# A two-layer decoder trunk on one core: the boundaries between sub-layers taken by token halves

## What is computed

```python
def rms_norm(x, g):
    y = x * lax.rsqrt(jnp.mean(x * x, axis=-1, keepdims=True) + NORM_EPS)
    return y * g

def swiglu(h, w_in, w_out):              # D_FF = 2816
    gu = h @ w_in
    gate, up = gu[..., :D_FF], gu[..., D_FF:]
    return (jax.nn.silu(gate) * up) @ w_out

for i in range(DEPTH):                   # DEPTH = 2
    f = swiglu(rms_norm(h, norm_pre[i, 0]), w_ffn_in[i, 0], w_ffn_out[i, 0])
    h = h + 0.5 * rms_norm(f, norm_post[i, 0])
    t = rms_norm(h, norm_pre[i, 1])
    t = attention(t) if i == 0 else conformer_conv_module(t)
    h = h + rms_norm(t, norm_post[i, 1])
    f = swiglu(rms_norm(h, norm_pre[i, 2]), w_ffn_in[i, 1], w_ffn_out[i, 1])
    h = h + 0.5 * rms_norm(f, norm_post[i, 2])
```

## Time and profile before

| | us |
|---|---|
| median of 3 runs | 1892.01 (1891.94 to 1893.06) |
| the profiled execution | 1891.92 |
| its span, first to last instruction | 1890.0 |
| PE busy | 1869.1 (99%) |
| weight loads of PE busy | 1542.6 (82%) |
| DVE busy | 1005.7 (53%) |
| ACT busy | 634.6 (34%) |
| POOL busy | 28.0 (1%) |

### The profile page before, as it was taken

How to read it: one execution, slowest core, us unless ns; L and a number is a source line. 1 busy time by engine, 2 the same in 40 slices (tenths; PEclk the granted TensorE clock), 3 DMA queues, 4 the chain that set the end, 5 groups by cost and what they waited for, 6 DMA issues and landing times.

```text
span 1890.0 us, 24212 instructions
## 1 busy us (share of the span) xinstructions
PE 1869.1 (99%) x8970; PEld 1542.6 (82%) x8970; DVE 1005.7 (53%) x1377; ACT 634.6 (34%) x920; POOL 28.0 (1%) x54
## 2 busy tenths in 40 slices
PE   8999999999999999999999999999999999999998
PEld 6888888887688888888888888888998888888886
DVE  5534434588766434444754344457767674344345
ACT  5322322446734222223442222234113543222223
POOL 0000000021000000000000000000000000000000
PEclk9999999999999999999999999999999999999999
DMA  5332223321023322323232232332332222322221
GB/s 189 111 100 100 89 100 100 114 84 62 14 88 100 100 90 99 100 90 106 72 122 90 99 101 90 99 111 76 124 121 96 89 78 89 100 100 96 94 100 56
DMA packets 62096, 181.49 MB, mean 96 GB/s; under 512 B 7088, under 2 KB 16448, under 8 KB 62032
## 3 DMA queue, kind: packets, MB, share of 16 engines
q1 hardware_dynamic: 60432, 179.09, 28.2%
q0 software_dynamic: 1600, 1.51, 0.3%
HBM read 173.63 MB, written 6.29 MB: 95 GB/s over the span
## 4 chain that ended last, share of the span: by engine, by line
PE 96%; DVE 2%; ACT 1%; DMA 1%; issue 0%; SPq 0%; DVEq 0%; ACTq 0%
PE bank L362 27%; PE bank L364 27%; PE bank L363 27%; PE bank L662 3%; PE bank L403 3%; PE bank L404 2%; PE bank L407 2%; PE bank L379 1%; PE bank L611 1%; PE bank L595 1%; PE bank L386 1%; PE bank L576 1%; DVE h_resid L1088 0%; DVE f_out L1083 0%; PE bank L552 0%
## 5 line engine op out<-in xcount | busy, mean ns | idle before, releaser
L977 DVE TENSOR_TENSOR w_lo<-w_raw,w_hi 128x1024 fp32r<-128x1024 f32 x307 | 375.3, 1225 | 449.0 <-ACT w_hi L745 438.6
L362 PE MATMUL bank<-x_hi,w_hi 128*128 128x512 f32 x1448 | 565.7, 391 | 0.8 <-DVE gate_tmp L1013 0.2
L364 PE MATMUL bank<-x_hi,w_lo 128*128 128x512 f32 x1448 | 563.5, 389 | 0.0
L363 PE MATMUL bank<-x_lo,w_hi 128*128 128x512 f32 x1448 | 563.4, 389 | 0.0
L745 ACT ACTIVATE w_hi<-w_raw 128x1024 fp32r<-128x1024 f32 x307 | 322.9, 1055 | 598.8 <-PE bank L364 596.8
L362 PE MATMUL bank<-a_hi,w_hi 128*128 128x512 f32 (+1 forms) x844 | 320.7, 380 | 0.4 <-DVE w_lo L977 0.4
L362 PEld LDWEIGHTS bank<-x_hi,w_hi 128*128 128x128 f32 x1448 | 271.8, 188 | 59.0 <-DVE gate_tmp L1013 2.1
L364 PE MATMUL bank<-a_hi,w_lo 128*128 128x512 f32 (+1 forms) x844 | 319.9, 379 | 0.0
L363 PE MATMUL bank<-a_lo,w_hi 128*128 128x512 f32 (+1 forms) x844 | 319.9, 379 | 0.0
L364 PEld LDWEIGHTS bank<-x_hi,w_lo 128*128 128x128 f32 x1448 | 271.8, 188 | 56.7
L363 PEld LDWEIGHTS bank<-x_lo,w_hi 128*128 128x128 f32 x1448 | 271.9, 188 | 55.6
(11 more groups left out here) (167 smaller groups left out, 1261.7 us busy)
## 6 DMA issues: line engine op xcount, KB each, us to landing
w_raw<-stream SPq DMA_DIRECT2D x312, 512.0 KB, 3.4
h_resid<-xT SPq DMA_DIRECT2D x8, 256.0 KB, 6.8
w_raw<-stream SPq DMA_DIRECT2D x8, 256.0 KB, 6.4
u_scratch<-V SPq DMA_DIRECT2D x8, 256.0 KB, 2.1
u_groups<-u_scratch SPq DMA_DIRECT2D x8, 256.0 KB, 2.8
qT<-z_scratch SPq DMA_DIRECT2D x8, 256.0 KB, 3.8
outT<-h_resid SPq DMA_DIRECT2D x8, 256.0 KB, 2.2
z_scratch<-kT SPq DMA_DIRECT2D x4, 256.0 KB, 2.3
```

The lines of the kernel that those rows point to most:

```text
L362: nc.tensor.matmul(out, lw[0], lx[0], start=first, stop=False)
L363: nc.tensor.matmul(out, lw[0], lx[1], start=False, stop=False)
L364: return nc.tensor.matmul(out, lw[1], lx[0], start=False, stop=last)
L977: nc.vector.tensor_tensor(w_lo[:, s, :], raw[:, s, :], w_hi[:, s, :].bitcast(F32), ALU.subtract).then_inc(s_lo, 1)
```

## The change

The last two down slots of every sub-layer but the last are made in the order: slot 7 tokens A (0 to 255), slot 8 A, slot 7 tokens B (256 to 511), slot 8 B (`last_two`), A in banks 6 and 7, B in banks 0 and 1. The sums of squares of the post norm, their root, the inverse and the broadcast are made for A and for B apart, those of A between products of the B halves, those of B between upper products of A of the next sub-layer (`first_four`). DVE scales and adds all eight chunks of A, then all eight of B, each 256 wide, and only then makes all `x_lo`, then adds the squares. PE makes the hi by hi and lo by hi products of the next four slots for all of A, then for all of B, then the products with `x_lo`, 512 wide. Of these four slots the third and fourth lie in two side buffers, `side_hi` and `side_lo`, since the ring places are still in use by the last two down slots. The four slots write banks 6, 7, 2 and 3. The filler matmuls of the boundaries are gone. The sums for `r_pre` are made in slot five ahead of its chunk 3, its broadcast ahead of its chunk 6; DVE adds the last square too, so there are four summing matmuls in place of eight. `u_groups` is laid into `a_lo`, to make room; its memset moves behind the last down slot ahead of the convolution.

On PE, with the buffers:

```diff
+        side_hi, side_lo = sb("w_side_hi", [P, 2, SLOT], F32R), sb("w_side_lo", [P, 2, SLOT], F32R)
...
-        ug = sb("u_groups", [P, 2, GROUPS, PAD + NT])
+        al = a_lo[:, :, :].bitcast(F32).rearrange("p a n -> p (a n)")
+        ug = al[:, 0:2 * GROUPS * (PAD + NT)].rearrange("p (i g n) -> p i g n", i=2, g=GROUPS)
...
+            def first_four(n0, sub):
...
+                def upper(k, tok):
+                    for s in range(RING):
...
+                        for part in range(2):
+                            nc.tensor.matmul(bank[FIRST_BANKS[s]][:, tok], w[KD * s + k][part], x_hi[:, k, tok],
+                                             start=(k == 0 and tok == A and part == 0), stop=False,
+                                             skip_group_check=True)
...
+                for k in range(KD):
+                    pe.wait_ge(s_xa, KD * (sub - 1) + k + 1)
+                    upper(k, A)
+                    if k == 1:
+                        post_columns(sub - 1, 1)
+                    if k == 4:
+                        pe.wait_ge(s_diag, 3 * sub)
+                        pe.wait_ge(s_evac, n0)
+                        broadcast(BCAST_B, range(NB // 2, NB)).then_inc(s_bc, 1)
+                for k in range(KD):
+                    pe.wait_ge(s_xhi, KD * sub + k + 1)
+                    upper(k, B)
+                for k in range(KD):
+                    pe.wait_ge(s_x, KD * sub + k + 1)
+                    for s in range(2):
+                        last = lower(s, k)
...
+                for s in range(2, RING):
+                    for k in range(KD):
+                        last = lower(s, k)
+                    last.then_inc(s_mm, 1)
...
             def first_body(n0, sub):
...
+                for s in range(2):
+                    n = n0 + RING + s
+                    pe.wait_ge(s_lo, n + 1)
...
+                    for k in range(KD):
+                        if (s, k) == (0, 3):
...
+                            pe.wait_ge(s_hacc, (KD - 1) * (sub + 1))
+                            add_columns(f[:, 0, :], True, True).then_inc(s_stat, 1)
+                        if (s, k) == (0, 6):
...
+                            pe.wait_ge(s_diag, 3 * sub + 1)
+                            broadcast().then_inc(s_bc, 1)
+                        last = x_block(s, k)
...
+            def last_two(n0, sub, blocks=KD):
...
+                for i in range(2):
+                    s = 2 + i
+                    pe.wait_ge(s_lo, n0 + 7 + i)
+                    for k in range(blocks):
+                        last = mm3(bank[A_BANKS[i]][:, HALVES[0]], (blk(w_hi, s, k), blk(w_lo, s, k)),
+                                   (a_hi[:, k, HALVES[0]], a_lo[:, k, HALVES[0]]), k == 0, k == blocks - 1)
+                    last.then_inc(s_mm0, 1)
+                pe.wait_ge(s_evac, n0 + 6)
+                for i in range(2):
+                    s = 2 + i
+                    for k in range(blocks):
+                        last = mm3(bank[B_BANKS[i]][:, HALVES[1]], (blk(w_hi, s, k), blk(w_lo, s, k)),
+                                   (a_hi[:, k, HALVES[1]], a_lo[:, k, HALVES[1]]), k == 0, k == blocks - 1)
+                        if (i, k) == (0, 3):
...
+                            post_columns(sub, 0)
+                        if (i, k) == (1, 0):
+                            pe.wait_ge(s_diag, 3 * sub + 2)
+                            pe.wait_ge(s_rpre, sub + 1)
+                            broadcast(BCAST, range(NB // 2)).then_inc(s_bc, 1)
+                    last.then_inc(s_mm, 1)
...
-                    keep_warm(3)
...
-                    keep_warm(10)
```

On ACT:

```diff
             def boundary(sub, n0):
...
+                root_of(3 * sub + 2, slice(0, NB // 2))
+                for k in range(KD):
+                    act.wait_ge(s_ha, KD * sub + k + 1)
+                    x_part(sub + 1, k, HALVES[0], s_xa)
+                    if k == 1:
+                        for i in range(2):
+                            act.wait_ge(s_evac, n0 - 1 + i)
+                            nc.scalar.activation(sq[:, i, HALVES[1]], f[:, 6 + i, HALVES[1]], ACT.Square
+                                                 ).then_inc(s_fsq, 1)
+                    if k == 3:
+                        root_of(3 * sub + 3, slice(NB // 2, NB))
                 for k in range(KD):
                     act.wait_ge(s_h, KD * sub + k + 1)
-                    x_chunk(sub + 1, k)
-                root_of(2 * sub + 3)
+                    x_part(sub + 1, k, HALVES[1], s_xhi)
+                for k in range(KD):
+                    h_square(k)
                 next_slot(n0, 0, n0 // RING)
+                next_slot(n0 + 1, 1, n0 // RING)
+                root_of(3 * sub + 4)
+                next_slot(n0 + 2, 2, n0 // RING)
                 keep_r_pre(sub + 1)
```

On DVE, and the scratch size at the end:

```diff
+            def side_slot(n0, i):
+
+                dve.wait_ge(s_hi, n0 + 3 + i)
+                nc.vector.tensor_tensor(side_lo[:, i, :], raw[:, 2 + i, :], side_hi[:, i, :].bitcast(F32), ALU.subtract
+                                        ).then_inc(s_lo, 1)
...
+            def boundary(sub, n0, how):
+
+                A, B = HALVES
+                invert(3 * sub + 2, slice(0, NB // 2))
+                dve.wait_ge(s_bc, 3 * sub + 2)
                 for k in range(KD):
+                    scale_by_rms(k, A, BCAST)
+                    add_residual(sub, k, A, s_ha)
+                    if k == 1:
+                        for i in range(2):
+                            dve.wait_ge(s_mm, n0 - 1 + i)
+                            to_f(B_BANKS[i], 6 + i, how, B).then_inc(s_evac, 1)
+                        add_half_square(sub, 1)
+                    if k == 4:
+                        invert(3 * sub + 3, slice(NB // 2, NB))
+                dve.wait_ge(s_bc, 3 * sub + 3)
+                for k in range(KD):
+                    scale_by_rms(k, B, BCAST_B)
+                    add_residual(sub, k, B, s_h)
+                for k in range(KD):
+                    x_lo_of(sub + 1, k)
+                for k in range(1, KD):
+                    add_h_square(sub + 1, k)
+                    if k == 3:
+                        next_slot(n0, 0)
+                next_slot(n0 + 1, 1)
+                invert(3 * sub + 4)
+                next_slot(n0 + 2, 2)
...
+    nc = bacc.Bacc("TRN2", target_bir_lowering=False, num_devices=1, dynamic_dma_scratch_size=4096)
```

More of the change, by code:

```diff
@@ L336, in _ @@
             pool.dma_start(conv_c[:, :], conv_in[:, :]).then_inc(s_const, 16)
-            for i in range(2):
-                nc.gpsimd.memset(ug[:, i, :, 0:PAD], 0.0).then_inc(s_zeros, 1)
             def swap(c, x):
@@ L379, in add_columns, with broadcast, four_slots @@
                     ins = nc.tensor.matmul(STAT[:, t:t + 1], src[:, t * P:(t + 1) * P], ones[:, 0:1],
-                                           start=(first and t == 0), stop=last, skip_group_check=True)
+                                           start=(first and t == blocks[0]), stop=last, skip_group_check=True)
                 return ins
-            def broadcast():
-                for t in range(NB):
-                    ins = nc.tensor.matmul(BCAST[:, t * P:(t + 1) * P], r_col[:, t:t + 1].broadcast_to([P, P]),
+            def broadcast(out=BCAST, blocks=range(NB)):
+                for t in blocks:
+                    ins = nc.tensor.matmul(out[:, t * P:(t + 1) * P], r_col[:, t:t + 1].broadcast_to([P, P]),
                                            ident[:, :], start=True, stop=True)
                 return ins
-            def four_slots(n0, blocks, hi_ready, lo_ready, before_last, among_last):
-                x = {KD: (x_hi, x_lo), -KD: (a_hi, a_lo)}[blocks]
+            def four_slots(n0, x, out, hi_ready, lo_ready):
                 for k in range(KD - 1):
@@ L443, in body, with bodies @@
                 last.then_inc(s_mm, 1)
-            def bodies(n0, count):
-                with pe.Fori(0, count // RING) as i:
+            def bodies(n0, count, done=0):
+                for s in range(done, RING if done else 0):
+                    body(n0 + s, s)
+                with pe.Fori(1 if done else 0, count // RING) as i:
                     for s in range(RING):
@@ L477, in down @@
                         down_slot(RING * i + (n0 + s), s, blocks, ready if s == 0 else None)
-                if final:
+                if final and sub < SUBS - 1:
+                    for s in range(2):
+                        down_slot(n0 + KD - RING + s, s, blocks)
+                    last_two(n0, sub, blocks)
+                elif final:
                     for s in range(RING - 1):
@@ L766, in sqrt_table, with pair_steps @@
                 nc.scalar.activation(tiny[:, 0:1], eps[:, 0:1], ACT.Sqrt)
[L768 removed]
+            def pair_steps(n, s, turn, q, chunk, first=False, second=True):
                 if not first:
@@ L1012, in scale_to, with pair_steps @@
                     dve.wait_ge(s_rpre, rpre)
```

(12 more changed lines are left out.)

352 lines of the change are left out of this document (182 added, 170 removed).

## The result

| | us |
|---|---|
| before, median of 4 runs | 1892.18 (1891.94 to 1893.06) |
| changed, median of 4 runs | 1879.62 (1879.10 to 1882.08) |
| ratio, with its 95% interval | 0.9937 (0.9926 to 0.9949) |
| the profiled execution, changed | 1880.11, span 1878.2 |

What follows compares the result with a forecast made beforehand. PE, busy 99% of a 1890.0 us span, was taken to bound the kernel, with gains only between sub-layers. Boundaries 14.9 + start 0.55 - convolution wait 2.7 = 12.8 us gained, giving 1879.1, stated as 1879.2 us; range 1876.2 to 1885.5.

Steps and rivals of the forecast that it cites:

- Part 1: At the five boundaries, token halves remove the 5.90 us gap and fillers: 9.41 us becomes 6.40, together 14.9 us gained.
- the fp32 groups: Summing matmuls and broadcasts between products at each boundary, charged 5.13 us in all after the change.
- four summing matmuls, I take 1.02: At boundaries, a group of four sums costs half of 1.83 us plus 0.1 for going to fp32 and back.
- part 2: In the boundaries, PE does not wait for DVE and ACT: cost 0, bounds 0 and 1 us per boundary.
- The cut: At boundaries, splitting a 512-wide product into two 256-wide halves costs 0.0127 us more.
- Rival B: In the five boundaries, the DVE-ACT chain paces PE, losing 1 us each: 1884.2 us; chance 0.16.
- Part 3: At the program's start, cheaper sums and broadcast, less a 0.5 us wait for slot five's weights: 0.55 us gained.
- Part 4, the convolution: Before the first group convolution, the later r_pre makes PE wait 2.7 us, once; bounds 0 and 4.
- Part 4, QKV at nothing: In QKV, the later r_pre delays DVE 3.4 us at most; charged 0, bound 2.1.
- rival C: In QKV, the late factor also turns into a wait: 2.1 us more, 1881.3 us; chance 0.07.
- Rival A: No convolution wait, sums halving cleanly at boundaries: 1874.6 us at best, 1876.5 if only the wait falls; chance 0.10.
- Rival D: In the first four slots, half-wide products are dearer, at 0.188 us each 43.7 us more: 1922.9 us; chance 0.03.

Runs made afterwards that it cites:

- e4: Kernel before, its order kept, with upper products of the four side-by-side slots cut into 256-column halves (392 cuts): 1896.66 us.
- e7: Changed kernel with VectorE making each x_lo of the second token half right behind the next chunk's residual, between FFN stages: 1890.92 us.
- e1: Changed kernel with two convolution slots computed one step earlier, ahead of the convolutions of channel blocks 0 and 1: 1876.64 us.
- e2: Changed kernel with the fourth ring slot's weight conversions (ScalarE and VectorE) done ahead of the factor's copy into r_pre: 1878.43 us.
- e3: Changed kernel with the factor for the stage behind a boundary broadcast two chunks (1.36 us) later in slot five: 1884.92 us.
- e10: Changed kernel with the fourth slot converted ahead of the factor, plus seven filler products before the first group convolution: 1876.50 us.
- e9: Changed kernel with seven filler products added at the start of the attention, where TensorE waits: 1880.10 us.
- e6: Kernel before without the 3 and 10 filler products in each of the first five boundaries: 1904.80 us.

## Why the prediction was right, point by point

**Part 1, the gap, right; the fp32 groups, mis-sized.** The step "four summing matmuls, I take 1.02" measures 0.81 (370.79 to 371.60) and 0.08 for the slower first product behind it, 0.89. "A broadcast of two, 0.57" measures 0.36 and 0.08, 0.44. The sums of B took 0.99 and 0.11; 0.18 of it is no cost of the group, but a wait for x (see part 2). The last sums and the broadcast of four take 0.81 each and 0.1. In all about 4.7 where 5.13 was charged, so 3.4 per boundary; the marks give 3.36 to 3.50. The order within that is not as forecast: boundaries 1 and 4, with eight chunks, give 3.47 and 3.50, and boundary 2, with six, 3.36, where 2.93 and 3.01 were laid out. Why is open. I had left half a switching cost on every group; the rows show that it belongs to the first product behind it and is a tenth of a microsecond. The cut was priced right, by e4 too. The layout of part 2 gave the same group of four sums 0.90, from 5.75 to 6.65, where the sum of part 1 charged 1.02; 0.90 was the better.

**Part 2, no wait of PE in the boundary, right but for 0.2 us.** The upper products began at 374.99, 9.96 us after the mark; 10.2 was laid out. At A the chain is as thin as I made it. ACT's parts of the first and the third chunk of A:

```profile
374.37 0.51 ACT L835 ACTIVATE x_hi<-h_resid,cols 128x256 fp32r<-128x256 f32 x1 [2.33 <-DVE h_resid L1198]
...
377.38 0.51 ACT L835 ACTIVATE x_hi<-h_resid,cols 128x256 fp32r<-128x256 f32 x1 [1.04 <-DVE h_resid L1198]
```

The first is ready at 374.88, 0.11 before PE takes it. The third is ready at 377.89, and PE, through with the sums of B, starts on it at 377.94, 0.18 later than behind the sums of A: the copying out of B on DVE stands ahead of it. From there on DVE's 0.85 a chunk against PE's 0.96 and the broadcast build a reserve, 1.2 us where B begins, and e7 shows what happens when it is used up. Rival B, with 0.16, was not far off at A and far off at B.

**Part 3, the start.** 0.44 by the marks against 0.55, which the spread of that stretch does not tell apart. Slot five waits for `w_lo`: it starts at 33.77 in place of 33.18, 0.59 late, and its first product takes 0.1 more, against 0.5 expected. The two fp32 groups take 0.90 each there, so 2.5 us in place of the 3.01: 0.5 gained by the rows.

**Part 4, the convolution, right: 2.64 against 2.7.** The rows that answer to the earlier trace rows, on DVE and PE:

```profile
1317.28 1.12 DVE L1351 SCALAR_TENSOR_TENSOR V<-up_tmp,cols,gate_tmp 128x512 f32<-128x512 f32 x1 [0.79 <-ACT gate_tmp L1025]
1318.24 3.88 DVE L1364 TENSOR_TENSOR f_out<-conv_consts,taps 128x1152 f32<-128x1152 f32 x3
```

```profile
1319.73 6.27 PE L744 MATMUL bank<-a_lo,f_out 128*128 128x128 f32 x54 [2.64 <-DVE f_out L1364]
```

e1 removes it and 2.85 of the stage. Luck had a part: in the profiled execution the clock held behind this wait, and fell behind waits of 2.10 and 4.00 at the same place. By the 1.65 us of e2 a fall would make it about 1881.3, an estimate. One of the four executions of the changed kernel took 1882.08 us with a mean granted clock of 0.996, the other three 1879.10 to 1880.11 with 0.997 and 0.998.

**Part 4, QKV at nothing: the step that failed.** "PE asks for a bank four slots later ... so I charge 0, bound 2.1." I looked at when QKV's products need banks and weights, and that was right: PE has no wait in QKV. But the attention behind it is paced by DVE and ACT, and takes their backlog with it. It cost 3.4 - 0.94 = 2.5 us, a little over the bound. e3 shows it from one side: 1.36 us later factor, 1.38 longer stage. e2 shows it from the other: 2.1 back. That is rival C's lateness, which had 0.07 and 2.1 us, though the wait came in the attention and not in QKV. The edit of e2 moved one conversion of 1.06 us on ACT and one of 1.23 on DVE, and DVE's wait for the swap shrank by 0.8; how the 2.1 divides between the two conversions was not taken apart.

**The sum.** Against the forecast: boundaries +2.2 (17.1 in place of 14.9, with 3.4 taken for the two whose stage holds more than a boundary), attention -2.5, convolution with its restart -0.1, start -0.1. That the first two cancel is luck. A right time does not prove its working; the stages do.

**Rival A** came half: the fp32 groups were cheaper by the 0.4 us per boundary that it named, and the wait at the convolution came whole. Its argument, that the 0.79 before a gate is partly a table load, does not hold: before the second gate DVE waits 0.79 as well, and ACT has no table load there, only the 0.72 us of the sigmoid.

**Rival D** did not appear. Halves alternating four weight buffers keep 0.12 us, with the clock at 1.00 over them:

```profile
378.00:381.00 3.00, 3.00 (x25) 3.00 (x26) 2.89 (x9) 1.83 (x5) 0.74 (x1) 1.00 0.00 0
```

## What to carry to other kernels

When a change makes one factor later, follow it past the stage that first uses it, to the next stage that the slower engines pace: here lateness passed through a stage that TensorE bounds and came out in one that it does not, 1.38 us for 1.36. Price a wait of TensorE with the clock behind it, and put real products into it if there are any, fillers if not. Check a right total by stages, for errors of both signs hide in it.

## What was not expected of the hardware

The clock fell to its lower level in some idle stretches of TensorE and not in others, and their length alone does not say which: it fell behind waits of 2.10 and 4.00 us ahead of the convolution and 2.2 ahead of the attention, and held behind 2.64 ahead of the convolution and 2.30 ahead of the attention. Executions of one and the same kernel differ in it as well (e2, 0.998 and 0.999 in the mean). What decides is not settled by these runs. Where TensorE was the pace, a fall cost 1.65 to 1.7 us (e2 against e10); in the kernel before without fillers 2.3 to 3.6 in each of the five stages behind the start. Where it was not the pace, it cost nothing (e1, e9).

The clock column does not show everything. At the program's start the changed kernel's products start 0.43 us apart (9.35, 9.77, 10.20), the pace that belongs to a clock of 0.50 in e6, and the window from 8 to 12 us reads 1.00.
